# SSD's group seams and its last group: another pair of PSUM banks for a group's first projection, and DeltaNet's first Q projection ahead of the transposes

## The reference

```
xbc = silu(_dwconv_centred(xbc, ssd_conv_w, ssd_conv_b))      # x, B and C of SSD, 5 taps
y   = y_f + flip(y_b) + ssd_d * xs                            # two directions of the chunked scan
y   = _rms((y * silu(z_s)).reshape(..., SSD_GROUPS, 512))     # normalized inside each group
u_s = (y * ssd_norm_w) @ w_ssd_out
...
qkv = silu(_dwconv_centred(qkv, gdn_conv_w, gdn_conv_b))      # q, k, v of DeltaNet, 5 taps
```

## Time and profile before

| what | value |
| --- | --- |
| median of 3 runs | 2110.86 us (2107.85 to 2114.84) |
| the profiled execution's own time | 2107.91 us |
| its span | 2106.0 us |
| TensorE matmul busy | 1876.8 us, 89% of the span |
| VectorE (DVE) busy | 1006.4 us, 48% |
| ScalarE (ACT) busy | 511.8 us, 24% |
| GpSimd (POOL) busy | 358.9 us, 17% |
| mean granted TensorE clock | 0.953 of full |

### The profile page before, as it was taken

The page is one execution under the profiler, slowest core; times in us unless marked ns, Lnnn a source line. Parts: engine busy times, 40 slices in busy tenths (PEclk is TensorE's granted clock), DMA queues, the critical chain, the costliest instruction groups (busy, mean ns, idle before and its releaser), DMA issues. The chain is left out here.

```text
span 2106.0 us, 31191 instructions
## 1 busy us (share of the span) xinstructions
PE 1876.8 (89%) x12670; PEld 1095.9 (52%) x12670; DVE 1006.4 (48%) x1859; ACT 511.8 (24%) x1420; POOL 358.9 (17%) x350
## 2 busy tenths in 40 slices
PE   5988998989989999999999989999999993975796
PEld 2554544545456676666666665555555543322232
DVE  4657666576666657666666671000000366221125
ACT  1142342424333443433434331000000000110111
POOL 0224152440421111211211101000000010311110
PEclk9999999999999999999999999999999995887998
DMA  9334042431111110110101014334510556799984
GB/s 333 114 85 135 17 114 90 110 110 41 50 58 33 28 44 29 46 44 16 48 26 46 14 48 152 130 130 150 160 51 0 210 204 269 262 417 391 414 344 166
DMA packets 162240, 270.28 MB, mean 128 GB/s; under 512 B 13544, under 2 KB 124937, under 8 KB 147121
## 3 DMA queue, kind: packets, MB, share of 16 engines
q1 hardware_dynamic: 155352, 252.84, 34.7%
q0 software_dynamic: 4928, 10.50, 1.4%
q10 hardware_dynamic: 1816, 4.94, 0.6%
HBM read 252.27 MB, written 22.27 MB: 130 GB/s over the span
## 5 line engine op out<-in xcount | busy, mean ns | idle before, releaser
L751 PE MATMUL bank<-hT,shared 128*128 128x512 f32 x368 | 179.5, 616 | 0.0
L1596 PE MATMUL bank<-hT,shared 128*128 128x512 f32 x352 | 157.5, 601 | 9.1 <-DVE xT L1923 9.1
L1630 PE MATMUL bank<-kept,hT 128*128 128x512 f32 x320 | 147.3, 597 | 0.0
L2094 DVE SCALAR_TENSOR_TENSOR prod<-gth,bank 128x512 f32<-128x512 f32 x16 | 11.0, 688 | 268.9 <-PE bank L2068 268.9
L1596 PEld LDWEIGHTS bank<-hT,shared 128*128 128x128 f32 x352 | 66.3, 194 | 86.7 <-issue 86.7
L2068 PE MATMUL bank<-yT,wm 128*128 128x512 f32 x256 | 111.2, 592 | 0.0
L1089 ACT COPY DT<-bank 128x512 f32<-128x512 f32 (+1 forms) x120 | 61.8, 515 | 198.1 <-PE bank L851 197.1
L1827 POOL TENSOR_TENSOR M<-M,pen 128x1024 f32<-128x1024 f32 x40 | 103.1, 2597 | 20.6 <-DMA M<-runs 20.6
L1754 ACT ACTIVATE M<-M,ST 128x128 f32<-128x128 f32 x320 | 97.0, 388 | 27.1 <-POOL M L1827 27.1
L1881 DVE SCALAR_TENSOR_TENSOR kept<-spadded,scw,kept 128x644 f32<-128x644 f32 x96 | 99.2, 1033 | 3.4
L2068 PE MATMUL bank<-hT,wm 128*128 128x512 f32 x224 | 97.9, 595 | 3.1 <-DVE prod L2096 3.1
(11 more groups left out here) (434 smaller groups left out, 3495.6 us busy)
## 6 DMA issues: line engine op xcount, KB each, us to landing
shared<-in_w_in_dram SPq DMA_DIRECT2D x58, 512.0 KB, 5.5
M<-runs SPq DMA_DIRECT2D x40, 512.0 KB, 6.9
kept<-in_w_ada_dram SPq DMA_DIRECT2D x8, 2048.0 KB, 13.6
ring<-in_w_exp_gate_dram SPq DMA_DIRECT2D x12, 1024.0 KB, 14.3
ring<-in_w_exp_up_dram SPq DMA_DIRECT2D x12, 1024.0 KB, 18.5
ring<-in_w_exp_down_dram SPq DMA_DIRECT2D x12, 1024.0 KB, 19.0
kept<-in_w_exp_down_dram SPq DMA_DIRECT2D x10, 1024.0 KB, 14.4
aw<-in_w_ada_dram SPq DMA_DIRECT2D x8, 1024.0 KB, 21.2
```

What stands on the lines that cost most here:

```text
L751: last = pe.matmul(bank[LATB[j]][:, :], wof(j)[:, k, :], hT[:, k, SEQ:T], start=(k == 0), stop=(k == KD - 1), skip_group_check=True)
L1596: pe.matmul(bank[a][:, :], wn(n)[:, k, :], hT[:, k, SEQ:T], start=(k == 0), stop=(k == KD - 1))
L1630: last = pe.matmul(bank[Z[t % 2]][:, :], hT[:, k, t * P:(t + 1) * P], wz[:, k, :], start=(k == 0), stop=(k == KD - 1), skip_group_check=True)
```

## The change

For groups after the first, n = 0 goes into banks 0 and 1 and no longer into 6 and 7. So PE's wait ahead of it is no longer for the last `beyond` (`s_yoffkept`) but for the last gate (bank 4 and 0, `s_zs`) and the last but one `keep_y` (bank 1, `s_ykept`). The first transpose, which writes bank 0, also waits until `raw` of n = 0 has emptied it. In the last group, Q's latent projection for DeltaNet's head 0 runs behind K's, into bank 6, and DeltaNet's own first steps leave it out.

```diff
                 for j in (K, Q):
-                    for i in range(4 if j == K else 0, 5):
+                    for i in range(4, 5):
                         if i == 4 and j == Q:
                             pe.wait_ge(s["g_raw"], 1)
                         proj(0, j, i)
...
         OUT = ((6, 7, 0), (5, 4, 0), (6, 7, 0), (0, 1, 0), (2, 3, 0), (0, 1, 0))
+        out = lambda g, n: (0, 1, 0) if n == 0 and g > 0 else OUT[n]
...
-                def proj(n, done=0):
-                    a, b, at = OUT[n]
+                def proj(g, n, done=0):
+                    a, b, at = out(g, n)
...
                     if g < SG - 1:
                         pe.wait_ge(s["s_bcin"], 32 * g + 32)
-                        pe.wait_ge(s["s_yoffkept"], 8 * g + 8)
-                        proj(0)
-                        proj(1)
+                        pe.wait_ge(s["s_zs"], 5 * g + 5)
+                        pe.wait_ge(s["s_ykept"], 5 * g + 4)
+                        proj(g + 1, 0)
+                        proj(g + 1, 1)
                     if g == SG - 1:
                         pe.wait_ge(s["s_next"], 64)
                         for k in range(KD):
                             pe.matmul(bank[5][:, :], w6[:, 1, k, :], hT[:, k, SEQ:T], start=(k == 0), stop=(k == KD - 1))
+                        pe.wait_ge(s["s_yoffkept"], 8 * g + 8)
+                        for k in range(KD):
+                            pe.matmul(bank[6][:, :], w6[:, 2, k, :], hT[:, k, SEQ:T], start=(k == 0), stop=(k == KD - 1))
                     for t in range(NT):
                         pe.wait_ge(s["s_yn"], 5 * g + t + 1)
+                        if t == 0 and g < SG - 1:
+                            pe.wait_ge(s["s_raw"], NJ * g + NJ + 1)
                         if t == 4 and g < SG - 1:
                             pe.wait_ge(s["s_raw"], NJ * g + NJ + 2)
...
-                    a, b, at = OUT[n]
+                    a, b, at = out(g, n)
                     act.copy(padded[:, n % 3, 2:2 + SEQ], bank[b][:, at:at + P])
                     act.copy(padded[:, n % 3, 6 + SEQ:6 + T], bank[a][:, :]).then_inc(s["s_raw"], 1)
```

More of the change, by code:

```diff
@@ L1651, in yoff @@
                         pe.matmul(bank[YOFF + d][:, :], CT[:, t, :], state[:, d, :], start=True, stop=True).then_inc(s["s_yoff"], 1)
-                proj(1, KD)
+                proj(0, 1, KD)
                 for g in range(SG):
@@ L1657, in _ @@
                     pe.wait_ge(s["s_raw"], NJ * g + 1)
-                    proj(2)
+                    proj(g, 2)
                     if g > 0:
                         pe.wait_ge(s["s_group"], g)
-                    proj(3)
+                    proj(g, 3)
                     pe.wait_ge(s["s_raw"], NJ * g + 3)
@@ L1665, in _ @@
                     cbs(g, 0)
-                    proj(4)
+                    proj(g, 4)
                     turn(g, 2, 1)
                     pe.wait_ge(s["s_raw"], NJ * g + 4)
-                    proj(5)
+                    proj(g, 5)
                     turn(g, 3, 2)
```

## The result

The changed kernel is slower: 2123.0 us median (2117.2 to 2128.7, 8 runs) against 2111.9 us (2107.9 to 2114.8, 8 runs), a ratio of 1.0058 with a 95% interval of 1.0043 to 1.0073. Of 2112 us that is 12 us, 9 to 15; the medians stand 11.0 us apart. The direction and the range were right, the size was not: the forecast of 2117 stood 6 us over the median.

The account below looks back on a forecast made before the run. PE, through the start of its transposes at each seam, was taken to pass delays on. Terms of -1.5, +4.5, +3.55, -0.49 and +2.1 summed to +8.2 us; between 2116.1 (profiled) and 2119.1 (median) it chose 2117, range 2109 to 2124.

Parts of the forecast that it names:

- the convolution now meets all four additions: Seams: DVE's convolution, issued sooner, is held by POOL's additions and ends 12.3 us from POOL's start.
- The added waits: Seams: new waits on gate and keep_y are met early; the one for raw of n = 0 costs nothing.
- The wait of 4.6 us: First seam: PE waits 4.6 us behind its projections for the scaled y, replacing waits of 3.05 and 0.79 us.
- The gain of 1.5 us: Three seams: the convolution ends sooner by 0.7, 0.4 and 0.4 us, in sum 1.5 us.
- The clock, put at 1.5 us a seam: Seams: low clock behind PE's longer wait slows transposes and next x projection; bounds 0 and 2.7, three seams 4.5 us.
- The wait ahead of V: DeltaNet: PE, with Q's projection gone, idles 6 us or more between Q's context part and raw of Q.
- The step to K's transposes: DeltaNet's start: raw of Q no longer waits 0.49 us for PE; low clock at V's parts costs 2.1 us.
- the clock term: DeltaNet: low clock at V's parts behind PE's idle time, 2.1 us, bounds 0 and 2.7.
- The sum: Whole kernel: -1.5 + 4.5 + 3.55 - 0.49 + 2.1 = +8.2 us on the profiled 2107.9 us.
- The first: Rival: low clock does not come or falls into idle time; +1.6 us, 2110 to 2112; chance 0.14.
- The second: Rival: seams' convolution isn't held by POOL; kernel 10 us faster, 2098 to 2101; chance 0.06.
- The third: Rival: seams as forecast, last group costs nothing; +2 us, 2110 to 2113; chance 0.06.

Follow-up runs that it names:

- r1_before: The kernel before, unchanged, profiled a second time; one run, 2108.2 us.
- m1_seams_busy: Only the seams' part of the change, plus five idle matmuls in PE's wait at each seam; 1.0009 against the kernel before.
- e3_busy_waits: The changed kernel plus five idle matmuls at each seam and five ahead of V's context part; 1.0021 against the kernel before, 4 us slower.
- e5_pool_last: Only the seams' part of the change, with POOL's four large additions behind the fifth scaling; 0.9930 against the kernel before, 15 us faster.
- e2_q_only: The kernel before with only the last group's part, Q's latent matmuls ahead of the transposes; 1.0011, 2 us slower.
- m2_all_v_busy: New banks, POOL's additions behind the fifth scaling, Q's projection in three pieces, five idle matmuls ahead of V's context part; 0.9924 against before, 16 us faster.
- e6_pool_last_old_banks: The kernel before, old banks, with only POOL's large additions held behind the fifth scaling; 1.0006, no difference.
- e4_pool_behind: The changed kernel with POOL's large additions at a seam behind the convolution of n = 0; 1.0046 against the kernel before, 10 us slower.

## Why the prediction was right or wrong

**The seams: the mechanism right, a size a little small.** "So the convolution now meets all four additions": it was issued with the first one and ended 12.3 us from POOL's start, as worked out. The added waits cost nothing. The wait of 4.6 us measured 4.87. The term was +3.0 us (-1.5 and +4.5), and the means of three profiles give +3.4, or +4.2 without r1_before. The gain of 1.5 us is seen in m1_seams_busy, 1.3 us. The clock, put at 1.5 us a seam, measured 1.4 to 2.1 us: the transposes took 3.79 to 4.53 us in the three profiles of the changed kernel, 2.40 without it. e3_busy_waits and m1_seams_busy show that the clock is its price; e5_pool_last shows that POOL's additions are what pins the convolution and the scalings.

**The last group: right in the profile, less in the runs.** The transposes started 3.5 us later, and the barrier with them. raw of Q no longer waited for PE. The wait ahead of V was 5.22 us and not 6 or more, since Q's context part in front of it had itself waited 0.90 us for raw of K, which I had left out. The step to K's transposes was forecast at +1.6 us (-0.49 and +2.1) and measured +2.2 against the first profile of before in each of the three after, +2.6 against the mean of before; the clock term was a little small. e2_q_only put a smaller time on this part, 0 to 5 us.

**What failed: from the sum to the time.** The sum was +8.2 us on the profiled execution, and then came the step "The median of the runs shown is 2110.9, so 3 us higher, which would give 2119.1; I put the time between the two, at 2117". That halved the offset and left a forecast of 6 us over the median, of which 11 to 12 were measured. A change has to be added to the same statistic that it is compared with. The full sum on the median would still have been 3 to 4 us short. By the timed runs the split was off too: the seams' part alone cost 9.5 us (5.9 to 12.9) where the sum had 3.0, and the last group's part 2 us (-0.4 to 5) where it had 5.2. The two errors cancel in part, so that the sum came nearer to the 12 us than its parts allow; that much was luck.

**What the sum lacked.** By the table the terms that I had came out at +8.8 us, and +4.7 us lie outside them: +4.0 in the groups, +2.1 ahead of the first seam, -1.3 behind. The prediction priced the low clock behind the waits that the change makes longer and nowhere else. It also took the waits of before from one profile, in which two of the three of 3.05 us went unpunished; in r1_before none did.

The +4.0 us in the groups is this clock as well: the time of the three groups, less half of the low-clock time in which PE was busy there, is 295.2 to 296.8 us in all sixteen profiles, whatever the kernel, while the groups themselves took 296.4 to 307.7. That low-clock time was 3.2 us in the mean of the three profiles of before and 11.4 in those of the changed kernel; half the difference is 4.1 us. So a term that my sum put at nothing measured +4.0 us, and its cause is the clock; what is open is why more of it falls there.

Inside a group PE also waits 1 to 3 us at a time, and whether such a wait is followed by a low-clock stretch changes when the group begins elsewhere: the changed kernel's third group (from 482 us) had two of them in each of its three profiles and was 1.5 us longer than in the first profile of before, the kernel before had one or none. What of the +4.0 us belongs to the change is not settled. For it: the seams' part alone was 9.5 us slower with 3.9 in its seams, and level with its waits filled. Against it: with the waits filled the groups kept 1.7 us, e5_pool_last and m2_all_v_busy, with no wait at the seams at all, had 2.5 and 2.8 us more, and e6_pool_last_old_banks, with old banks and short waits, had 5.6 us more in its groups.

The +2.1 us ahead of the first seam is in part (some 1 us, by 87 us of the span) older than any changed instruction; it is no low-clock time on a busy PE, of which both kernels have 18 us there in the mean. Why it is larger in the mean is open; the profiles overlap, with 195.7 to 197.1 us for the old banks and 197.0 to 200.0 for the new.

**The rivals.** The first (no low clock) is out, by the 3.8 to 4.5 us of the transposes. The second (taps not held by POOL) is out as a description of this kernel, and its price was nearly right: without POOL beside them the seams became 5.8, 5.4 and 5.4 us shorter, where it had 5.3 and twice 5.0 us. The third (the last group costs nothing) is out by the barrier's 3.5 us.

## What to carry to other kernels

An earlier start of a link in a chain gains nothing where the next link is held by something with a time of its own; here POOL's additions, started by another chain, held five taps and five scalings of DVE one by one. Move the intruder behind the chain's last instruction, not behind its first: one link short, the stall only moved on, and the kernel stayed 10 us slower, where it was 15 us faster with the additions behind the last (the slower one carries the last group's part as well, which cost 2 us alone). And work moved into a wait must fit the wait: eight matmuls in a gap of 3.16 us delayed a barrier, while two there and four in the next gap gained. Stretches that a change doesn't touch can still differ, as the groups did by 4.0 us, so measure them too; a single profile of before doesn't show which waits are punished in the next run.

## What the runs showed of the hardware

Scalings of y with one SBUF input (480 ns alone) were held by POOL's additions like the taps with two: median 2566 ns in e4_pool_behind, here over the five of the first seam (ns min/median/max):

```profile
L1974 DVE TENSOR_SCALAR ysum<-ysum,ysc x5: 482/2566/2580, 215.6 to 223.5; 128x512 f32<-128x512 f32 x5
```

At the seams one tap or scaling passed between two additions, never two.

Not every DVE instruction is held. Those with one input in a PSUM bank were not: four of the 32 products of L1923 in the first profile of before ran beside an addition, and all 32 took the same time, while the four sums of L1926 beside an addition, with both inputs in SBUF, took 2.0 us instead of 0.69:

```profile
L1923 DVE TENSOR_TENSOR xT<-bank,scur x32: 691/692/693, 167.0 to 580.0; 128x512 f32<-128x512 f32 x32
L1926 DVE TENSOR_TENSOR ysum<-ysum,xT x32: 691/692/2019, 167.7 to 580.8; 128x512 f32<-128x512 f32 x32
```

Idle matmuls of 4.46 us in waits of 4.9 to 5.2 made the kernel faster by about 8 us over four places (e3_busy_waits), and the granted clock stayed at 1.00 behind them; in its profile 2.1 us of the gain were K's convolution. In one place, ahead of V in m2_all_v_busy, they gained nothing that the runs could tell.

The low clock is not found behind long waits alone. In DeltaNet a wait of only 1.12 us in each head is followed by a stretch of it in some profiles and not in others; in the first profile of before the heads came 85.4 us apart with it, and in e5_pool_last the first four, without it, 83.7 us. By my estimate from these two, seven such heads make up to 12 us. That is near the scatter of the kernel before (2098 to 2113 us over 30 runs on one chip), though no run shows that this is all of it.
